# A state layer, its gated projection and four norms: an order of instructions changed in many places

## The reference

```python
for i in range(2):
    h = rmsnorm(x, norm_mix[i])
    y = S5(h) if i == 0 else HGRN2(h)      # each with its states
    x = x + y
    x = x + PEER(rmsnorm(x, norm_ffn[i]))  # 16384 one-neuron experts, 8 heads, top 16
return rmsnorm(x, norm_final), states
```

```python
s[t] = ab * s[t-1] + bb @ u[t]                 # complex, per group
y = Re(c @ s) + d * u
z = gelu(y) @ w_glu                            # 1024 x 2048
out = z[:, :1024] * sigmoid(z[:, 1024:])
```

## Time and profile before

| | |
|---|---|
| runs, us | 2148.07, 2147.36, 2148.16; median 2148.07 |
| profiled execution | 2148.27 us, span 2146.2 us |
| busy | PE 1898.0 us (88%), DVE 1669.7 (78%), ACT 1271.0 (59%), POOL 584.7 (27%) |
| mean granted TensorE clock | 0.925 of full |
| state layer's table and loop | 52 to 207 us of the span |
| gated projection | 228.3 to 277.8 us |
| second norm to first query scores | 277.8 to 301.8 us |
| HGRN output projection, fourth norm, wq1's start | 1309.7 to 1356 us |

### The profile page before, as it was taken

One profiled execution on the slowest core, in us unless ns is written; L12 is line 12 of the kernel. 1 busy time (PEld: TensorE's weight loads), 2 busy tenths in 40 slices (PEclk: granted clock), 3 DMA queues, 4 the chain that ended last, 5 costly groups with the idle time before them and its releaser, 6 DMA issues. The chain is left out here.

```text
span 2146.2 us, 48842 instructions
## 1 busy us (share of the span) xinstructions
PE 1898.0 (88%) x17676; PEld 1620.5 (76%) x17676; DVE 1669.7 (78%) x3261; ACT 1271.0 (59%) x2613; POOL 584.7 (27%) x475
## 2 busy tenths in 40 slices
PE   1253789899999999999988799999999999999998
PEld 0242667788888888888866656677888898888887
DVE  8879658978889788889844644788788997887896
ACT  3532468756565565656588454886665655556554
POOL 6474047600000022213257400773000000221240
PEclk7555899999999999999999957999999999999999
DMA  2000434555555588889854204345555566888894
GB/s 87 6 1 2 133 108 148 162 184 177 175 177 205 167 295 297 300 279 329 298 205 148 67 3 167 120 156 176 178 176 176 173 209 214 302 296 283 306 332 167
DMA packets 107550, 396.30 MB, mean 185 GB/s; under 512 B 12976, under 2 KB 12976, under 8 KB 107056
## 3 DMA queue, kind: packets, MB, share of 16 engines
q1 hardware_dynamic: 88416, 318.37, 43.1%
q0 software_dynamic: 19024, 76.59, 11.6%
HBM read 388.72 MB, written 6.19 MB: 184 GB/s over the span
## 5 line engine op out<-in xcount | busy, mean ns | idle before, releaser
L229 ACT ACTIVATE wsp<-ring 128x512 f16<-128x512 f32 x1200 | 750.9, 629 | 624.6 <-PE ps L292 612.7
L290 PE MATMUL ps<-hs,wsp 128*128 128x256 f16 (+1 forms) x2752 | 766.5, 279 | 67.4 <-POOL wsp L240 31.0
L291 PE MATMUL ps<-hs,wsp 128*128 128x256 f16 (+1 forms) x2752 | 766.3, 278 | 0.0
L292 PE MATMUL ps<-hs,wsp 128*128 128x256 f16 (+1 forms) x2752 | 766.0, 278 | 0.0
L290 PE MATMUL ps<-hT,wsp 128*128 128x256 f16 x2048 | 559.1, 273 | 6.3 <-DVE hT L1735 6.3
L292 PE MATMUL ps<-hT,wsp 128*128 128x256 f16 x2048 | 559.0, 273 | 0.0
L291 PE MATMUL ps<-hT,wsp 128*128 128x256 f16 x2048 | 559.0, 273 | 0.0
L242 DVE SCALAR_TENSOR_TENSOR wsp<-ring,wsp 128x512 f16<-128x512 f32 x560 | 374.5, 689 | 134.4 <-ACT wsp L229 132.6
L290 PEld LDWEIGHTS ps<-hs,wsp 128*128 128x128 f16 x2752 | 270.7, 98 | 126.4 <-POOL wsp L240 33.0
L249 DVE SCALAR_TENSOR_TENSOR wsp<-ring,wsp 128x1024 f16<-128x1024 f32 x216 | 264.2, 1224 | 102.8 <-ACT wsp L229 98.8
L240 POOL TENSOR_TENSOR wsp<-ring,wsp 128x512 f16<-128x512 f32 x208 | 272.3, 1329 | 175.3 <-ACT wsp L229 174.1
(11 more groups left out here) (294 smaller groups left out, 2041.9 us busy)
## 6 DMA issues: line engine op xcount, KB each, us to landing
ring<-in_v SPq DMA_DIRECT2D x256, 512.0 KB, 5.8
ring<-in_ub SPq DMA_DIRECT2D x216, 512.0 KB, 3.8
ring<-in_ua SPq DMA_DIRECT2D x40, 512.0 KB, 4.0
ring<-in_wq SPq DMA_DIRECT2D x32, 512.0 KB, 3.6
ring<-in_win SPq DMA_DIRECT2D x32, 512.0 KB, 3.7
ring<-in_glu SPq DMA_DIRECT2D x16, 512.0 KB, 3.7
big<-in_hgs POOLq DMA_DIRECT2D x1, 4096.0 KB, 13.0
ring<-in_wout SPq DMA_DIRECT2D x8, 512.0 KB, 4.4
```

The costliest lines, as they stand in the source:

```text
L229: nc.scalar.activation(wsp[:, k % 2, 0, cols], ring[:, k, cols], ACT.Copy, scale=scale).then_inc(hi_ready, 1)
L290: nc.tensor.matmul(out, w_hi, hi, start=start, stop=False, **kw)
L291: nc.tensor.matmul(out, w_hi, lo, start=False, stop=False, **kw)
L292: return nc.tensor.matmul(out, w_lo, hi, start=False, stop=stop, **kw)
```

## The change

Six things are done.

1. `project`: where the activations come in chunk by chunk, the first two blocks are done together: high x high and low x high of block 0 for all chunks, the same of block 1, then high x low of block 0 and of block 1. The waits are for `hs_hi`, and later for `hs_lo`. `norm_dve` makes all eight normalised chunks, then the low parts. This concerns the gated projection, wq0, win, wout and wq1.
2. Norms 1 and 3: ScalarE squares chunks inside the projection ahead, TensorE sums them after blocks (five sums before the last block's end, three after).
3. Table: 12 pairs for ScalarE instead of 14 (`AG = 6`), VectorE's last sums over pairs 12 to 31, GpSimd's over 0 to 11.
4. The first two gated blocks are split before the pair loop; the low part of `k0` comes before the wait for the table, and the first three `b_products` no longer wait for it.
5. In the pair loop `scan_out(d - 1)` comes before `x_lo(d - 2)`; five chunks get their GELU on ScalarE inside the loop, three between sample parts, the sample tokens last.
6. A sample step is three instructions of 256 columns and two of 128, instead of eight of 128.

```diff
 def project(...):
+            def first_two():
+                for k in range(2):
+                    wait_bank(0, k, True)
+                    for c in range(KC):
+                        if k == 0:
+                            pe.wait_ge(hs_hi, KC * inputs + c + 1)
+                        if c % 4 == 0:
+                            lo_half_done(pe, name, 0, k, c // 4)
+                        for f in range(2):
+                            nc.tensor.matmul(zbank(k, n), part(k, f, c), hs[:, 0, c, 0:n], start=(c == 0 and f == 0),
+                                             stop=False)
+                for k in range(2):
+                    for c in range(KC):
+                        if k == 0:
+                            pe.wait_ge(hs_lo, KC * inputs + c + 1)
+                        mm = nc.tensor.matmul(zbank(k, n), part(k, 0, c), hs[:, 1, c, 0:n], start=False,
+                                              stop=(c == KC - 1))
+                        if c % 4 == 3:
+                            mm.then_inc(used, 1)
...
+        def norm_square(act, k, c, done):
+            act.wait_ge(done, c + 1)
...
+            nc.scalar.activation(dst, src, ACT.Square).then_inc(norm_sq, 1)
+        def norm_sum(pe, k, c, start):
+            pe.wait_ge(norm_sq, c + (KC * k + 1))
+            return nc.tensor.matmul(norm_bank(k), ones[:, :], squares[:, ds(c, 1), :].rearrange("p o t -> p (o t)"),
+                                    start=start, stop=False, skip_group_check=True)
 def norm_act(act, k, following=None):
+            if k in (1, 3):
+                nc.scalar.activation(small[:, 176 + k:177 + k], epsc[:, 0:1], ACT.Sqrt)
+                for c in range(7 if k == 1 else 6, KC):
+                    norm_square(act, k, c, glu_x if k == 1 else hg_x)
 def norm_pe(pe, k):
+            if k in (1, 3):
+                for c in range(6 if k == 1 else 5, KC):
+                    mm = norm_sum(pe, k, c, False)
 def norm_dve(v, cnt, k):
-                if before and c >= 2:
-                    low(c - 2)
             if before:
-                low(KC - 2)
-                low(KC - 1)
+                for c in range(KC):
+                    low(c)
...
-        AG = 7
+        AG = 6
...
+                    if lev >= WIDE:
+                        q = slice(AQ, PAIRS)
                     table_sums(nc.vector, q, w, lambda ins: ins.then_inc(s5_tab_addv, 1))
...
-                    table_sums(nc.gpsimd, slice(AQ, HQ), w, done)
...
 def s5_prepare_act(act):
+            for k in range(2):
+                split_hi(act, "glu", 0, k)
             s5_table_act(act)
 def s5_pairs_pe(pe):
-            pe.wait_ge(s5_dve, DVE_K0)
-            pe.wait_ge(s5_pool, POOL_ZX)
             for d in range(DUOS):
                 b_products(d)
+                if d == 3:
+                    pe.wait_ge(s5_dve, DVE_K0)
+                    pe.wait_ge(s5_pool, POOL_ZX)
 def s5_pairs_act(act):
                     x_hi(d - 2)
+                if d >= 7 and d % 2:
+                    s5_gelu_act(act, (d - 7) // 2)
 def s5_pairs_dve(v, cnt):
-            table_done(v)
             k0_lo_dve(v)
...
+            for k in range(2):
+                split_lo(v, "glu", 0, k)
+            table_done(v)
...
                 mul_in(d)
+                if d:
+                    scan_out(d - 1)
                 if d >= 2:
                     x_lo(d - 2)
-                if d:
-                    scan_out(d - 1)
 def s5_sample_step(v, cnt, half, s):
+            cnt.add(tt(ta, arb, prev, ALU.mult))
+            cnt.link(tt(tb, aib, prev, ALU.mult))
+            cnt.link(tt(ta, ta, now, ALU.add))
+            for r, op in enumerate((ALU.subtract, ALU.add)):
+                tt(now[:, r], ta[:, r], tb[:, 1 - r], op).then_inc(s5_rec, 1)
 def s5_samples_dve(v, cnt):
             low(1)
-            for k in range(2):
-                split_lo(v, "glu", 0, k)
+        def s5_gelu_act(act, c):
+            act.wait_ge(s5_yp, y_done(c))
+            nc.scalar.activation(hT[:, c, 0:TP], hT[:, c, 0:TP], ACT.Gelu).then_inc(s5_g, 1)
 def s5_out_act(act):
+            s5_gelu_act(act, KC - 3)
             for half in range(2):
...
-                if half == 0:
-                    for k in range(2):
-                        split_hi(act, "glu", 0, k)
...
+                s5_gelu_act(act, KC - 2 + half)
             act.wait_ge(s5_yd, 1)
+            nc.scalar.activation(hT[:, :, TP:T], hT[:, :, TP:T], ACT.Gelu).then_inc(s5_g, 1)
+            act.wait_ge(s5_g, KC + 1)
             for c in range(KC):
...
                 high_part(c).then_inc(hs_hi, 1)
 def glu_pe(pe):
+            def after(i, k, first):
+                if k % 2 and not first:
+                    norm_sum(pe, 1, i * 2 + k // 2 - 2, i == 1 and k == 1)
 def glu_act(act):
                     nc.scalar.activation(sig[m], zbank(k), ACT.Sigmoid, scale=UNSC).then_inc(glu_sig, 1)
+                    if m or not first:
+                        norm_square(act, 1, i * 2 + m - 1, glu_x)
 def hg_act(act):
+            def post(i, k, first):
+                if i * 4 + k >= 2:
+                    norm_square(act, 3, i * 4 + k - 2, hg_x)
 def hg_pe(pe):
+            def after(i, k, first):
+                if i * 4 + k >= 3:
+                    norm_sum(pe, 3, i * 4 + k - 3, i * 4 + k == 3)
```

More of the change, by code:

```diff
@@ L294, in project, with part @@
         def project(pe, name, wait_bank, after=None, a=0, b=None, inputs=None, n=T):
-            def post(i, k, first):
[L298 to L306, removed]
+            def first_two():
+                def part(k, f, c):
+                    return wsp[:, k, f, c * P:(c + 1) * P]
+                for k in range(2):
[16 more added lines that the diff above has]
+                            mm.then_inc(used, 1)
+            def post(i, k, first):
+                if inputs is not None and first and k < 2:
+                    if k == 0:
+                        first_two()
+                else:
+                    wait_bank(i, k, first)
+                    for c in range(KC):
+                        if c % 4 == 0:
+                            lo_half_done(pe, name, i, k, c // 4)
+                        mm = three_passes(zbank(k, n), k % 2, c, hs[:, 0, c, 0:n], hs[:, 1, c, 0:n], c == 0, c == KC - 1)
+                        if c % 4 == 3:
+                            mm.then_inc(used, 1)
                 if after:
@@ L568, in tab_add_before @@
         def tab_add_before(lev):
-            return 2 * (min(lev, WIDE) - NARROW) + 6 * max(lev - WIDE, 0)
+            return 2 * (min(lev, WIDE) - NARROW) + 4 * max(lev - WIDE, 0)
         def table_sums(eng, q, w, done):
@@ L1048, in free @@
                     pe.wait_ge(glu_mul, i * 2 + k // 2 - 1)
-            project(pe, "glu", free, inputs=0)
+            def after(i, k, first):
+                if k % 2 and not first:
+                    norm_sum(pe, 1, i * 2 + k // 2 - 2, i == 1 and k == 1)
+            for trip in range(4):
+                project(pe, "glu", free, after, trip, trip + 1, inputs=0)
         def glu_act(act):
@@ L1966, in hg_act @@
                 high_part(c).then_inc(hs_hi, 1)
-            per_block(act, "wout", split_hi, lambda i, k, first: None, ahead=2, following=["wq1"])
+            def post(i, k, first):
+                if i * 4 + k >= 2:
+                    norm_square(act, 3, i * 4 + k - 2, hg_x)
+            per_block(act, "wout", split_hi, post, ahead=2, following=["wq1"])
         def hg_dve(v, cnt):
@@ L2180, in hg_pe @@
             pe.wait_ge(hg_h, HH)
-            project(pe, "wout", lambda i, k, first: None if first else pe.wait_ge(hg_x, i * 4 + k - 3), inputs=3)
+            def after(i, k, first):
+                if i * 4 + k >= 3:
+                    norm_sum(pe, 3, i * 4 + k - 3, i * 4 + k == 3)
+            project(pe, "wout", lambda i, k, first: None if first else pe.wait_ge(hg_x, i * 4 + k - 3), after, inputs=3)
         @block.sync
```

31 lines of the change are left out of this document (12 added, 19 removed).

## The result

The changed kernel takes 2136.93 us (median of 8 runs, 2135.13 to 2143.37) against 2148.11 of the kernel before (8 runs): ratio 0.995, interval 0.9941 to 0.9959, 11.2 us less. Forecast were 2144.2, in a range of 2139.0 to 2149.5; the gain is nearly three times the forecast one, and outside the range. By the 4.3 us that the prediction took as the least it could tell, the kernel is faster, for which it gave 0.40; it gave 0.48 to no change. The profiled execution has 2135.13 us, span 2133.4 against 2146.2, granted clock 0.927 against 0.925.

A forecast was written before the change was run, and what follows sets the result against it. Bound: six VectorE and GpSimd instructions taking turns in the pair loop, TensorE from 228.3 us on. Terms +1.5 - 0.8 - 4.7 + 0.3 + 1.2 - 1.9 + 0.3 = -4.1 took 2148.27 to 2144.2 us, range 2139.0 to 2149.5.

The forecast's parts named there:

- Scan ahead of `x_lo`: Pair loop: VectorE's new order makes the scan meet GpSimd's input sum; +1.5 us, bounds -1 to +4.
- the six file: Pair loop: six VectorE and GpSimd instructions run one after another through something both engines need, 6.10 us a duo before.
- 6.05 us, some 0.1 less: Pair loop: summed durations of a duo in the new order, less hidden start-up; 5.95 us against 6.10.
- The fill: Start of the pair loop: second scan no longer waits for the first `x_lo` and all ahead of it; -1.7 us.
- Sample steps: State layer: fewer, wider instructions save 0.1 us a step; -0.8 over eight steps, bounds 0 and -4.8.
- Tail: End of state layer: table load, GELUs and splits moved earlier, gated matmuls start sooner; -4.7 us, bounds -4.0 to -5.2.
- Table and splits: Table ahead of the loop: pairs about even, splits beside GpSimd's last sums may delay it; +0.3 us, bounds -0.3 to +1.3.
- Norms: Squares and sums between blocks: second norm -1.9 us, bounds -2.6 and -0.6; HGRN output +0.3.
- High parts first: Projection starts: ring slot free after 36 matmuls instead of 12; +1.2 us with the gated start, bounds -3 and +5.
- rival 2: Projection starts: four late slots lose 1.0 to 1.5 us more each, giving the gain back; 2148 us, chance 0.21.
- Rival 1: Pair loop: the port does not hold it, the reorder removes `x_lo`'s wait; -15.9 us, 2126.8, chance 0.09.
- rival 3: Pair loop: input products lose their cover and take turns with GpSimd's last sum; +16.8 us, 2161, chance 0.10.

The follow-up runs named there:

- the first experiment: Changed kernel with `x_lo` ahead of the scan again in the pair loop: median 2140.26 us, ratio to before 0.9967.
- c1: Second profile of the same changed kernel, no edit, taken with the experiments: span 2136.0 us.
- first profile: First profile of the changed kernel, no edit: 2135.13 us, span 2133.4.
- the two file experiments: Changed kernel with evacuation and memset between scan and `pout`: 2133.80 us; changed kernel with ScalarE zeros instead of VectorE's `x_lo`: 2126.78 us.
- the GELU experiment: Changed kernel with all eight chunk GELUs behind the last sample add again: median 2139.44 us, ratio to before 0.9959.

## Why the prediction failed, step by step

*Scan ahead of `x_lo`, forecast +1.5: wrong, −2.7 by the first experiment, and this is the step that failed.* The mechanism was right: the six file, the input products are in it and one sum is out, scans come in two distances in turn. Wrong was the term "6.05 us, some 0.1 less": a duo is 5.61. I added durations, undisturbed or nearly so but for `x_lo` (1.21, 1.24, 0.6, 1.2, 0.55, 1.25), where the file runs by distances between ends, which are 1.21, 1.06, 0.54, 1.13, 0.55, 1.12. The difference is 0.44 us, over four of the steps, and I had allowed 0.1. The distances are measured; that a waiting instruction has its start-up behind it when its turn comes is how I read them, and no run tests it. Rows of my own said so: GpSimd's product ends 1.12 after VectorE's, and I quoted that and then put 1.2 into the sum. Ten duos lose 2.7 us of forecast by it (59.2 against 61.9, the evacuation being 0.77 instead of 0.6 in the other direction), the duos with sample steps about 1.0. The fill was right (1.8, forecast 1.7); the last scan lost 1.5 (forecast 1.8). The distances 1.12 and 0.55, put in for every hand-over of the earlier trace rows, give 5.67 a duo, 2.8 us less over ten duos, and would have moved the range's lower end from 2139.0 to 2136.2, below the result.

*Sample steps, −0.8:* right; 0.15 each in the loop, 0.4 for the four behind it.

*Tail, −4.7:* right, 5.1 with its sample steps; GELUs and splits each showed their part when put back.

*Table and splits, +0.3:* +0.65 by the first scan's end from the span's start, and +0.06 without the splits: within the bounds, by the mechanism given, the case in which one split gets in first. The +0.4 and +0.8 of the table above are this and the first `std`'s own shift.

*Norms, −1.9 and +0.3:* right, about −2.3 and 0.0 to +0.4.

*High parts first, +1.2 in all:* the sum came out near 0 to +0.8. I took the clock as low for 5.9 us at wq0 and the first scores as 0.8 late; with 6.7 us (c1) they are 0.5 late, with 5.3 (first profile) 0.2 early. In the kernel with the evacuation moved it is low for 5.9, as before, and they are 0.13 late, so the term was some 0.7 too high. The gap over a microsecond ahead of the third block, which I named as rival 2's mark, is there (1.53 us idle) and does not decide, since the start is 1.65 sooner. As a mark it was badly chosen; the first scores were the one to read.

*Wq0's other 1.6 us* was in no step. The kernel before has the low stretch at 741.5 us in its profile and the two profiles of the changed one have not. No line of the change stands at that place; the stretch follows the idle time in five of twelve profiles. Whether it comes by chance in each execution or with a kernel's timing is not shown: the only kernel profiled twice lacks it both times. The Trainium skill (TensorE: Matmul & The Clock Gate, section "Part 1: The HAM clock gate (the "warmup" mystery)") calls the number of slow matmuls at a kernel's start variable from run to run; the windows above, one for each kernel and in the middle of a stage, fit that and do not show it.

So −4.1 became −10.2 in the second profile of the changed kernel: 4.4 from the loop and 1.9 from wq0, most of it the clock's. The loop's 4.4 alone would have left the time at 2139.8 us, inside the range; the low stretch that the kernel before has and the changed one lacks carried it out. Rival 1, "the port does not hold the loop", is refuted by the two file experiments although the time went its way; rival 3 is refuted by 669 to 692 ns.

## What to carry to other kernels

Where two engines take turns, sum the distances between successive ends in the trace, not the durations of single instructions, and shift work that does not need the shared resource into the waits: the evacuation did that for 3 us. A gain at the start of a stage counts only at the first point where another engine must catch up, so read that point (here the first scores). For effects of a few us, compare stretches between fixed events and count low-clock stretches before reading a median. Make sure that the later event follows the earlier one: the first scan did not follow the first `std`, and only the span's start showed the table's 0.65 us.

## What was not expected of the hardware

- A VectorE instruction that waits for GpSimd adds 0.54 us behind it where it takes 0.69 undisturbed, GpSimd's sum 1.06 where it takes 1.26; the record of the waiting one grows to 1.57 and 2.11, so busy time reads as 58.34 of 59.19 us for an engine that has room for 0.72 us more in a duo.
- The same idle stretch of 3.2 us is followed by 3.4 us at a granted clock of 0.51 in the profile of one kernel and at 1.00 in that of another: 19 against 34 matmuls.
- A table load moved out of the way by itself: 1.28 us in idle time ahead of the wait in the GELU experiment, behind the wait in the kernel before.
